# One diffusion step on one NeuronCore: SSD decay products as two fp32r passes instead of one fp32 product, and the state operand's product with C moved from GpSimd to VectorE

## The reference, cut to what matters

```python
A = a_dt of the chunk                       # step size times a, per token
A_cs = cumsum(A)
Lm = segsum_exp(A)                          # exp of the sums between two tokens, triangular
cb = einsum('bclgn,bcsgn->bgcls', C, B)
y_diag = einsum('bgrcls,bcsgrp->bclgrp', cb * Lm, X)
y_off = einsum('bclgn,bcgrpn,bgrcl->bclgrp', C, prev_states, exp(A_cs))
```

## Time and profile before

| | us |
|---|---|
| median of 3 runs | 2520.07 |
| lowest and highest | 2515.96, 2522.47 |
| the profiled execution, device time | 2515.34 |
| its span in the trace | 2513.5 |

### The profile page before, as it was taken

The page is one execution under the profiler, slowest core; times in us unless marked ns, Lnnn a source line. Parts: engine busy times, 40 slices in busy tenths (PEclk is TensorE's granted clock), DMA queues, the critical chain, the costliest instruction groups (busy, mean ns, idle before and its releaser), DMA issues.

```text
span 2513.5 us, 35187 instructions
## 1 busy us (share of the span) xinstructions
PE 2334.3 (93%) x14713; PEld 2026.9 (81%) x14713; DVE 1489.6 (59%) x2210; ACT 794.1 (32%) x1421; POOL 233.1 (9%) x257
## 2 busy tenths in 40 slices
PE   5999899988999898999999999899888999999998
PEld 3767857878888888779999999798555789999997
DVE  4376482357434777667565556788666486555654
ACT  4433332210131116344132223533555352222222
POOL 0022040023101330110000000200000110000002
PEclk9999999999999999999999999999898899999999
DMA  7401205520252011222132212122000022221321
GB/s 294 164 26 55 76 1 197 191 78 1 76 206 96 9 51 59 67 101 87 57 96 76 80 59 84 49 76 68 5 1 1 26 72 72 84 75 60 93 68 42
DMA packets 43852, 193.58 MB, mean 77 GB/s; under 512 B 5008, under 2 KB 5008, under 8 KB 36912
## 3 DMA queue, kind: packets, MB, share of 16 engines
q1 hardware_dynamic: 41472, 178.10, 21.3%
q0 software_dynamic: 2224, 13.24, 1.5%
HBM read 183.72 MB, written 7.60 MB: 76 GB/s over the span
## 4 chain that ended last, share of the span: by engine, by line
PE 81%; DVE 13%; issue 2%; ACT 2%; DMA 1%; SPq 0%; DVEq 0%; ACTq 0%
PE pg L836 29%; PE pg L873 16%; PE pg L631 16%; PE ps L782 3%; PE pg L1031 2%; PE ps L1051 2%; DVE att L1784 2%; PE ps L605 2%; DVE wk L1790 1%; PE pg L1006 1%; PE ps L725 1%; DMA ybuf<-in_wada 1%; PE ps L1006 1%; PE ps L729 1%; DVE tp L1788 1%
## 5 line engine op out<-in xcount | busy, mean ns | idle before, releaser
L836 PE MATMUL pg<-hh,xhi 128*128 128x320 f32 (+2 forms) x1008 | 313.7, 311 | 6.5 <-DVE hl L1604 6.5
L836 PE MATMUL pg<-hl,xhi 128*128 128x320 f32 (+2 forms) x1008 | 310.6, 308 | 0.0
L836 PE MATMUL pg<-hh,xlo 128*128 128x320 f32 (+2 forms) x1008 | 310.4, 308 | 0.0
L1490 DVE TENSOR_TENSOR wlo<-ring,whi 128x1024 fp32r<-128x1024 f32 x129 | 157.0, 1222 | 187.9 <-ACT whi L1091 187.7
L631 PE MATMUL pg<-hh,whi 128*128 128x320 f32 x976 | 239.3, 327 | 22.0 <-DVE hl L1522 9.6
L631 PE MATMUL pg<-hl,whi 128*128 128x320 f32 x976 | 225.4, 313 | 0.0
L631 PE MATMUL pg<-hh,wlo 128*128 128x320 f32 x976 | 224.9, 312 | 0.0
L631 PEld LDWEIGHTS pg<-hh,whi 128*128 128x128 f32 x976 | 165.5, 192 | 61.1 <-issue 50.3
L836 PE MATMUL pg<-hh,whi 128*128 128x320 f32 (+2 forms) x672 | 209.2, 311 | 3.3 <-DVE hl L1604 3.3
L836 PE MATMUL pg<-hh,wlo 128*128 128x320 f32 (+2 forms) x672 | 207.3, 308 | 0.0
L836 PE MATMUL pg<-hl,whi 128*128 128x320 f32 (+2 forms) x672 | 207.2, 308 | 0.0
(11 more groups left out here) (309 smaller groups left out, 4661.7 us busy)
## 6 DMA issues: line engine op xcount, KB each, us to landing
ring<-in_wstream SPq DMA_DIRECT2D x231, 512.0 KB, 3.7
adaring<-in_wada SPq DMA_DIRECT2D x21, 1024.0 KB, 5.0
ybuf<-in_wada SPq DMA_DIRECT2D x21, 1024.0 KB, 5.0
adabig<-in_wada SPq DMA_DIRECT2D x6, 1024.0 KB, 18.7
xk<-in_x SPq DMA_DIRECT2D x1, 2560.0 KB, 11.2
yssd_scratch<-ybuf POOLq DMA_DIRECT2D x2, 1280.0 KB, 6.2
xk<-yssd_scratch POOLq DMA_DIRECT2D x1, 2560.0 KB, 11.0
xk<-in_x_tok POOLq DMA_DIRECT2D x1, 2560.0 KB, 10.2
```

What stands on the lines that cost most here:

```text
L836: last = nc.tensor.matmul(out, w[:, k * P:(k + 1) * P], h[:, k, a:b], start=k == 0 and m == 0, stop=k == KT - 1 and m == 2)
L1490: V.tensor_tensor(lo, flat(ring[:, s % RING]), hi.bitcast(F32), ALU.subtract).then_inc(wlo_ready, 1)
```

## The change

The fp32 product of a matrix of ones with `ra` becomes two fp32r products that add up in PSUM: one with a rounded part `rah`, one with the rest `ral`. The matrices of ones are held once more as fp32r (`cmr`). The step sizes are split once for the whole kernel: `adth` is `adt` rounded to fp32r, `adtl` the rest. In each turn ACT makes `rah` (four scaled copies of the mask, 128x128 each, with a column of `adth` as the scale), and DVE makes `ral` as it made `ra`. PE waits for both. Finally the product of `ec` with C goes from POOL's program to DVE's, behind the product of `eg`. `rah` and `ral` lie in the memory of `xsT`.

```diff
+            adth = sb("adth", [P, TT, 32], F32R, ph)
+            adtl = sb("adtl", [P, TT, 32], F32, ph)
+            cmr = sb("cmr", [P, 3, P], F32R, ph)
...
-                        pe.wait_ge(ra_ready, v + 1)
-                        if v:
-                            pe.wait_ge(ex_ready, v)
-                        nc.tensor.matmul(ps[:, 0, :], cm[:, (GT, LT)[d], :], ra[:, d].rearrange("p h t -> p (h t)"),
-                                         start=True, stop=True).then_inc(dd_ready, 1)
-                        if v:
-                            pe.wait_ge(exc_ready, v)
-                        nc.tensor.matmul(ps[:, 1, :], cm[:, ONES, :], ra[:, d].rearrange("p h t -> p (h t)"),
-                                         start=True, stop=True).then_inc(dd_ready, 1)
+                        for bank, m, freed_by in ((0, 1 + d, ex_ready), (1, 0, exc_ready)):
+                            if v:
+                                pe.wait_ge(freed_by, v)
+                            for part, made, r in ((0, rah_ready, rah), (1, ral_ready, ral)):
+                                pe.wait_ge(made, v + 1)
+                                last = nc.tensor.matmul(ps[:, bank, :], cmr[:, m, :],
+                                                        r[:, d].rearrange("p h t -> p (h t)"),
+                                                        start=part == 0, stop=part == 1)
+                            last.then_inc(dd_ready, 1)
...
+                def step_sizes(n, d):
+
+                    (t, q), u = SSD_UNITS[n], g * len(SSD_UNITS) + n
+                    if u:
+                        act.wait_ge(dd_ready, 4 * (u - 1) + 2 * d + 2)
+                    for h in range(4):
+                        c = d * 16 + HPG * g + 4 * q + h
+                        last = nc.scalar.activation(rah[:, d, h], cm[:, (LE, GE)[d], :], ACT.Copy,
+                                                    scale=adth[:, t, c:c + 1].bitcast(F32))
+                    last.then_inc(rah_ready, 1)
+
+                act.wait_ge(cmr_ready, 1)
+                for d in range(2):
+                    step_sizes(0, d)
...
+                        if n + 1 < len(SSD_UNITS):
+                            step_sizes(n + 1, d)
...
-                    V.tensor_tensor(ra[:, d], per_head(a, P),
+                    V.tensor_tensor(ral[:, d], per_head(a, P),
...
+                        dve.wait_ge(exc_ready, 2 * u + d + 1)
+                        V.tensor_tensor(ecs[u % 2][:, d], ecs[u % 2][:, d],
+                                        bcT[:, 1, t * P:(t + 1) * P].unsqueeze(1).broadcast_to([P, 4, P]),
+                                        ALU.mult).then_inc(cs_ready, 1)
...
+                    link(V.tensor_copy(adth[:], adt[:]))
+                    V.tensor_copy(cmr[:, 0], cm[:, ONES, :])
+                    V.tensor_copy(cmr[:, 1:3], cm[:, GT:LT + 1, :])
+                    V.tensor_tensor(adtl[:], adt[:], adth[:].bitcast(F32), ALU.subtract).then_inc(cmr_ready, 1)
...
-                        pool.wait_ge(exc_ready, 2 * u + d + 1)
-                        G.tensor_tensor(ecs[u % 2][:, d], ecs[u % 2][:, d],
-                                        bcT[:, 1, t * P:(t + 1) * P].unsqueeze(1).broadcast_to([P, 4, P]),
-                                        ALU.mult).then_inc(cs_ready, 1)
```

More of the change, by code:

```diff
@@ L279, in hybrid_step @@
         with ExitStack() as ph:
+            with ExitStack() as over:
+                rah = sb("rah", [P, 2, 4, P], F32R, over)
+                ral = sb("ral", [P, 2, 4, P], F32R, over)
             xsT = sb("xsT", [P, 4, NT], F32, ph)
@@ L285, in hybrid_step @@
             st = sb("st", [P, 2, 4, 512], F32, ph)
-            ra = sb("ra", [P, 2, 4, P], F32, ph)
+            adth = sb("adth", [P, TT, 32], F32R, ph)
+            adtl = sb("adtl", [P, TT, 32], F32, ph)
+            cmr = sb("cmr", [P, 3, P], F32R, ph)
             eg = sb("eg", [P, 2, 4, P], F32, ph)
@@ L452, in hybrid_step @@
         cb_ready = sem("cb_ready")
-        ra_ready = sem("ra_ready")
+        rah_ready = sem("rah_ready")
+        ral_ready = sem("ral_ready")
+        cmr_ready = sem("cmr_ready")
         dd_ready = sem("dd_ready")
@@ L1714, in step_sizes @@
                         dve.wait_ge(dd_ready, 4 * (u - 1) + 2 * d + 2)
-                    a = adt[:, t, d * 16 + HPG * g + 4 * q:d * 16 + HPG * g + 4 * q + 4]
-                    V.tensor_tensor(ra[:, d], per_head(a, P),
+                    a = adtl[:, t, d * 16 + HPG * g + 4 * q:d * 16 + HPG * g + 4 * q + 4]
+                    V.tensor_tensor(ral[:, d], per_head(a, P),
                                     cm[:, (LE, GE)[d], :].unsqueeze(1).broadcast_to([P, 4, P]),
-                                    ALU.mult).then_inc(ra_ready, 1)
+                                    ALU.mult).then_inc(ral_ready, 1)
                 def add_output(n):
@@ L2089, in _ @@
                     G.dma_start(ssd_out[:, d, 512 * g:512 * (g + 1)], sfin).then_inc(sfin_out, 16)
-                for i, (t, q) in enumerate(SSD_UNITS):
-                    u = g * len(SSD_UNITS) + i
-                    for d in range(2):
-                        pool.wait_ge(exc_ready, 2 * u + d + 1)
-                        G.tensor_tensor(ecs[u % 2][:, d], ecs[u % 2][:, d],
-                                        bcT[:, 1, t * P:(t + 1) * P].unsqueeze(1).broadcast_to([P, 4, P]),
-                                        ALU.mult).then_inc(cs_ready, 1)
                 pool.wait_ge(yz_ready, g + 1)
```

## The result

The change took the median from 2520.28 us (2515.96 to 2522.47, four runs) to **2504.24 us** (2501.16 to 2505.10, four runs): a ratio of 0.9937, with a 95% interval of 0.9922 to 0.9952. The forecast was 2502 us, in a range of 2493 to 2512. The profiled execution took 2501.16 us for a span of 2499.0, where the one before had 2515.3 and 2513.5, so between the two profiles 14.2 us went, against 17.8 in the working and 16.0 in the medians. Beside the first four experiments one of the 15 runs of the kernel before took 4577.51 us; the ratios leave it out, the median of 2520.76 given there has it in.

A forecast was written before the change was run, and what follows sets the result against it. TensorE (PE) was taken as the bound, busy 93% of the span. Stretches -19.8, ahead +1.0, clock +1.0 sum to -17.8 us: 2497.5 from the profiled 2515.3, 2502 as median against 2520.07; range 2493 to 2512.

The forecast's parts named there:

- The product's price and VectorE's: Two fp32r products of 512 columns step by 0.23 us; VectorE's products by 0.61, 9.7 us per pair of units.
- ScalarE's copies: ScalarE's four copies making `rah`: 0.295 us each, 2.18 per direction, 8.7 per pair, hidden under 9.95.
- The pair: Two units in the steady part: 9.95 us instead of 12.8, so 5.7 us won in units 4 to 7.
- The start: Each group's head: eight copies delay the first exp 2.4 us; four directions at 2.18 then take 8.7.
- the lead at unit 4: From each group's start to unit 4's exps: 1.7 us ahead of before, despite the slow start.
- The clock: At each group's start, a fall makes a few products of units 0 and 1 take twice as long: +0.5 per group.
- Ahead of it: Before the first convolution, four small VectorE instructions splitting the step sizes, all on the path: +1.0 us.
- The signs that it named: Right: pairs 9.9 to 10.2 us, stretches 55 to 56, +1 us at 76 us. Wrong: granted clock under 0.95 in either stretch.
- two fp32r passes might step like one fp32 product: Rival on TensorE's decay products: only POOL's part won, 2510 us; near no change, 0.13 together with ScalarE bound at 0.48.
- ScalarE as the bound: Rival: copies at 0.35 us give 2505; at 0.48, pair 11.7 and total 2522, chance 0.13 shared with the last rival.
- VectorE slower than 0.61: Rival: every product waits and takes 0.69 us, pair 10.7 on VectorE, total 2508; counted within the forecast's 0.82.
- The clock that stays low: Rival: clock falls at the stretch's start and stays low, pair 17.4 us, 16 slower per group, about 2550; chance 0.05.

The follow-up runs named there:

- the first four experiments: Against the kernel before: product with C on VectorE, 2514.41 us; fp32r passes, 2512.61. Against the changed kernel: eight copies earlier, 2496.51; step-size split behind second convolution, 2503.23.
- the fifth copy: Changed kernel plus an unused 128-column ScalarE copy beside the four of each direction and unit: 2507.57 us.
- the copies moved: Changed kernel with ScalarE's first eight copies of each group ahead of the last gate tile's evacuation instead of behind it: 2496.51 us.
- own banks with the split kept: Changed kernel with first eight copies ahead of the last gate tile and direction 1's decays in two idle banks, step-size split ahead of first convolution: 2495.65 us.
- one pass: Changed kernel with the second decay pass left out; TensorE multiplies only rounded step sizes, rests made but unused: 2497.66 us.
- own banks: Changed kernel with first copies ahead of the last gate tile, split behind the second convolution, direction 1's decays in two idle banks: 2493.04 us.

## Why the prediction was right, and where its sizes were off

**The product's price and VectorE's.** Two fp32r passes at 0.23 us, VectorE at 0.60 to 0.61 per product, and 9.6 to 9.8 us of VectorE per pair (predicted 9.7): all as taken. **ScalarE's copies**, the term without a row, came out at steps of 0.29 us (predicted 0.295, ends 0.28 and 0.48), 2.14 us per direction (2.18), hidden in the pairs as foreseen; the fifth copy shows by how much.

**The pair** was mis-sized: 9.95 us forecast, 10.36 measured. The prediction had the decays of a unit done at 2.3 us; they took 2.55. It let all four products of a unit's direction step by 0.23 us. In the trace the first of them is followed after 0.31 to 0.34 us, so that the exponential starts 0.74 us behind it instead of 0.66, the second direction pays the same extra again behind its wait, and there is one more such step before the output products. Two units make +0.5, and the product of C and B took 0.25 instead of 0.33. From the exponentials of unit 4 to those of unit 8 the gain was 25.59 - 20.72 = 4.9 us, forecast 5.7; behind them 15.22 - 13.18 = 2.0, forecast 2.5.

**The start.** The copies' 2.4 us were right (the first exponential 4.54 us behind the product of C and B instead of 2.21, so +2.3), and the run with the copies moved confirms them. From there to the exponentials of unit 2 the forecast was 8.7 us, ScalarE's loop of four directions; 10.26 and 10.12 were measured. The second group of the kernel with the copies moved shows that way with no fall of the clock in it:

```profile
310.27:318.80 8.53, 6.06 (x34) 3.59 (x34) 7.21 (x13) 8.53 (x25) 0.00 (x0) 1.00 0.00 0
```

```profile
316.33 1.15 PE L753 MATMUL ps<-eg,rtb 128*64 128x128 f32 x16
317.40 0.49 PE L725 MATMUL ps<-bcT 128*128 128x128 f32 x2
```

ScalarE is busy all the time there and waits for nobody, and four directions take 8.53 us: the loop was sized rightly. In the change TensorE is at half clock, the sixteen output products take 1.97 us (174.13 to 176.10) instead of 1.07, the products of C and B and the decays behind them come late, and ScalarE waits 1.33 us (at 177.33). So what was missing up to unit 2 is the clock's 1.6 to 1.7 us. From the exponentials of unit 2 to those of unit 4 took 9.55 us, under the forecast 9.95. So the lead at unit 4 was 0.7 us (25.01 - 24.35), 0.8 in group 1, and not 1.7, or 1.2 with the 0.5 for the clock taken off.

**The clock** was the second term mis-sized. The fall that the prediction put at the start of the stretch did come, for 10.2 us in each group, and not for "a few products". What it cost down to unit 4 is not fully shown, since no kernel with the fp32r products went that far at full clock. From the first exponential to that of unit 4 the change takes 19.8 and 19.7 us (18.7 forecast); group 0 of the kernel with the copies moved, with one fall of 3.4 us, takes 19.1, by which the price is at least 0.5 to 0.7 per group, an estimate from these two kernels. Where a fall comes matters as much as its length: in group 1 of that kernel the 3.4 us at 325.2 came behind unit 2, among output products, after TensorE had waited 0.94 us for VectorE's rests; from unit 2 to unit 4 took 12.03 us there instead of 9.55, and the whole way 20.6. In sum a stretch won 7.6 and 7.7 us and not 9.9 less 0.5: of these 1.8 us per group, 0.8 are in the two pairs, 0.5 behind them, and 0.5 ahead of unit 4.

**Ahead of it** the split took 0.85 us of VectorE (four instructions from 70.34 to 71.19), as thought, and TensorE's wait grew from 1.30 to 2.10 us. But the stretch started 2.2 us late and not 1.0, with a fall of the clock at 77.7 us that the kernel before has not. Four of the seven kernels with the split in place have no such fall (those with the fp32r passes alone, the first copies moved, own banks with the split kept, one pass), though TensorE waits 2.09 or 2.10 us for `wlo` in them too, and they start at 160.93 to 161.30 us; the kernel with no split at all (the product with C alone) starts at 161.34. But the change and two others (the rounded step sizes on VectorE, the fifth copy) have it, at 77.5 to 78.8 us, and none of the five with a wait of 1.3 us has. So the split's wait does not bring the fall each time, and whether it makes it possible stays open. Over all ten kernels the start lies between 160.9 and 163.7.

**The sum** of the stages: -7.6 and -7.7 in the stretches, +2.2 ahead, -0.8 between the groups and -0.6 behind them, together the 14.5 us by which the span shrank. The stretches won 3.5 us less than forecast and the spot ahead cost 1.2 more; 1.4 came back elsewhere, for which the prediction had no term. The profiled execution of before took 2515.3 us at a mean granted clock of 0.975, 4.9 under the median, and that of the change 2501.16 us at 0.970, 3.1 under its own. That is why the medians (16.0) lie nearer to the forecast's 17.8 than the profiles do (14.2), and that part of the agreement is luck, as are the 1.4.

**The signs that it named.** The copies' fours (1.27 us), VectorE's products (0.68) and the first exponential (2.3 us later) came as it said. The pair (10.36, not 9.9 to 10.2), the stretches (58.3 and 58.1, not 55 to 56) and the spot ahead (2.2, not 1) did not, and one of its signs of being wrong did come: a granted clock of 0.91 in both stretches, where it had set 0.95. The main mechanism held, a pair bounded by TensorE and VectorE together with ScalarE's copies hidden; its sizes and the clock's part were less well known than the total suggests.

That two fp32r passes might step like one fp32 product was a rival too; the steps of 0.23 us above end it.

**The other rivals.** ScalarE as the bound fell by the fifth copy, in the pairs; it holds in the first two units alone, where it fills all of 8.53 us at full clock. VectorE slower than 0.61 fell by its rows. The clock that stays low didn't come: it is 1.00 in every steady window above, in all kernels, and every fall in a stretch begins less than 21 us behind its product of C and B, in the first four units. The section "A second HAM failure mode: psum-queue depth-cycling" of the Trainium skill, page "TensorE: Matmul & The Clock Gate", describes repeated falls in loops that wait for banks; the change has such a wait in every unit (0.23 and 0.22 us idle in a pair), and no window of its pairs shows a fall.

## What to carry to other kernels

- When two halves of a change relieve two engines that share a bound, the two alone show less than the whole (here 4.7 and 6.4 us of the stretches against 15.3): price the pair against all engines at once, and read which one fills the window.
- An idle engine's work is free only behind its first dependent: ScalarE's copies cost nothing in the steady pairs and 2.3 us at the stretch's head. Put the first round into the idle time ahead of the last thing that the loop needs. And behind such a change look at what TensorE still waits for: two idle banks were worth another 0.7 us per pair.
- A multiplication belongs to the engine with room in this window, whatever it is made for.

## What the runs showed of the hardware

- The first fp32r product of 512 columns behind a wait or another kind of product is followed after 0.31 to 0.34 us, the later ones after 0.23 (one of 0.26 behind each wait). Where the wait is gone (own banks, second direction) the extra goes too.
- The spread within one kernel goes mostly with the mean granted clock. The product with C alone gave 2511.82 and 2511.88 us at 0.973, 2513.66 to 2515.67 at 0.971, 2516.83 and 2516.91 at 0.969; the rounded step sizes on VectorE gave 2504.48 and 2505.35 at 0.973 and 2517.0 to 2519.3 at 0.964 to 0.966. By these, one thousandth of the clock goes with 1.3 us in the first kernel and 1.5 to 1.8 in the second, but not in each pair of runs: own banks gave 2493.31 us at 0.968 and 2492.60 and 2492.78 at 0.971. The profiled execution of the kernel with the rounded step sizes on VectorE (2504.48 us) has no stretch of 30.7 us at half clock where the profile of before has one from 1935.3 us and the change's from 1920.9; the code there is the same. The runs of one kernel spread by 1.4 to 14.8 us, so a difference of a few us between variants can be such falls, and only the stages of a trace tell them apart.
- Two-operand products of 512 columns on VectorE take 0.68 us alone and up to 1.77 us beside one of POOL's. In the trace of the kernel before, four `ra` in a row that began within 0.11 us behind a product of POOL ended 0.54 to 0.55 us behind that product's end (the first: POOL 163.68 to 164.96, VectorE 163.75 to 165.50), as if they had done most of their 0.68 us of work only then. POOL's own took 1.09 to 1.77 us; no run has one with VectorE idle, so what they lose is not known.
